# Last four value rows of each expert stage added by VectorE, and the first token tile turned before the last group's rows

## The chip, the core and the metric

One core of a Trainium2 chip runs the whole program once. The metric is device time of one launch in microseconds (us). The kernel before took 2772.89 us (median of three runs, 2770.57 to 2773.94).

## What is computed

Two blocks of a small language model, one after the other, on 256 tokens of width 1024, all in fp32. The first block has two layers; each ends in an expert stage (PEER) and a layer norm, and the change touches only these two ends:

```python
def peer_ffn(x, w_q, subkeys, u_tab, v_tab):          # 8 heads, 16 picks each, 16384 experts
    def block(xb):                                    # 128 tokens
        q = (xb @ w_q).reshape(n, PEER_HEADS, 2, PEER_HALF)
        s = jnp.einsum('nhpc,pkc->nhpk', q, sk)
        ...                                           # two rounds of top-16: eid, softmax weights gw
        u = u_tab[eid]
        act = jax.nn.gelu(jnp.einsum('nhkd,nd->nhk', u, xb))
        coef = gw * act
        return jnp.einsum('nhk,nhkd->nd', coef, v_tab[eid])
...
        y = peer_ffn(x, ...)
        x = layer_norm(DN_ALPHA * x + y, ln2_g[i], ln2_b[i])
```

After layer 0's stage (i = 0) comes the recurrent mixer of layer 1 (`rglru`); after layer 1's stage (i = 1) comes the first feed-forward of the second block (`ffn00`).

## The kernel before

**Tokens and groups.** The 256 tokens are two tiles of 128 (t = 0, 1). An expert stage runs 16 groups j (`NJ`): heads 0 to 7 of token tile 0, then of tile 1. A group has 16 picks k. For each pick one *u row* and one *v row* (128 tokens by 1024 numbers, 512 KB) are gathered by an indirect DMA that POOL issues (`pool_peer`, L1303). Each kind has a ring of 8 slots, so v row g may be issued only when row g - 8 is used up (label `v used g`).

**What each engine does with a row.** VectorE (DVE) takes the dot product of each u row with its token row (`dve_dots`, L1249). The token rows of tile 1 stand in PSUM, in banks 0 and 1 of `ps` (`x_row`). From 16 dots (in the last group: the first 8, then the other 8) come the GELU on ScalarE (ACT, L1154), the coefficients on DVE (`dve_coef`, L1262), and one 128x128 diagonal matrix per pick on ACT (`diag`, L1160). TensorE (PE) multiplies the diagonal by the v row into `acc` (`pe_peer`, L293): two halves of 512 columns, each fp32 product shown as two matmuls, so 4 matmuls in the trace per row.

**Order at the end of a stage.** POOL issues the v rows of a group mostly one group late; rows 8 to 15 of group 15 come after its last u row. PE works through rows 0 to 15 of group 15 in order. At k = 10 it turns token tile 0 of the next step (`pe_tokens`, 8 transposes, L1535), which was normalised in group 12. After row 15, DVE adds the sum to tile 1 (`dve_ln_sum`, L512), takes mean and variance, scales (L517 to L526), and PE turns tile 1. Before that, for i = 1, ACT and DVE make what the feed-forward needs of tile 0: high and low halves (L1544, L1554), the split of the first two weight chunks (L315, L323), and the mean square with its root (L1509, L1512, L1517).

**Order of weight loads.** SyncE (SP) loads weights in a fixed order; `r.x2` (i = 0) and `w1.00.1` (i = 1) are held until row 6 of group 15 is used (`HELD`).

**PSUM tiles.** All short-lived results of PE go through `open_tile`, which deals out the four banks of `ps` in turn: the tile number modulo 4 is the bank, and PE waits until the tile four numbers back has been read.

```python
i = len(tiles)
if i >= BANKS:
    pe.wait_ge(*by("read " + tiles[i - BANKS]))
```

Tiles opened ahead of group 15 of layer 0, by the code: setup 13 (`mem` 4, `kv0` 2, `x0` 4, `par`, `sd`, `sk`), the first mixer 40 (`m.gates`, `m.xq`, `m.0` to `m.5`, `m.col`, 8 of `m.G` and `m.S`, `m.6` to `m.11`, `xs0` 4, `m.N` 4, `xpT0` 4, `my` 3, `xo0` 2), tokens of `xp0` 4, `kv1` 2, and `pq0`/`ps0` 20 (heads 0 and 1 once for each token tile, heads 2 to 7 once): 79. From there to group 15 of layer 1 are 55 more: tokens of `xrt` 4, the second mixer 25 (`r.x` 4, `r.g` 8, `r.xq`, `r.gate` 4, `xs1` 4, `xpT1` 4) with `xo1` 2, tokens of `xp1` 4, `pq1`/`ps1` 20. The last four of a stage are heads 6 and 7 (`pq`, `ps`), long read by then.

Of the kernel before, what the change touches and what calls it, by code (L numbers as in the profile page):

```python
# [179 lines left out]
def build(nc, A, out, known):  # L180
# [9 lines left out]
    with ctx:  # L190
# [23 lines left out]
        def count_of(label):  # L214
            return by(label)[1]
# [54 lines left out]
        def open_tile(name):  # L270
# [5 lines left out]
            tile_bank[name] = i % BANKS  # L276
            return ps[:, i % BANKS, :]

        def tile_of(e, name):

            engine_of[e.who].wait_ge(pe_steps, count_of("tile " + name))
            return ps[:, tile_bank[name], :]
# [214 lines left out]
        def act_attention_out(i, m0):  # L497

            for pair in range(2):
# [7 lines left out]
        ln_bn, ln_ag, ln_std = (stat[:, 0:24].rearrange("p (t a b) -> p t a b", t=2, a=2),  # L507
                                stat[:, 24:28].rearrange("p (t b) -> p t b", t=2), stat[:, 28:30])

        def dve_ln_sum(t):  # L510

            dve.scalar_tensor_tensor(x_tok[:, t, :], x_tok[:, t, :], ALPHA, acc_rows(t), ALU.mult, ALU.add).then_inc(dve_steps, VE.step())  # L512
# [36 lines left out]
        def dve_peer_ln(i, t, part):  # L549

            g, b = f"ln2g{i}", f"ln2b{i}"
            if part == 0:
                dve.wait_ge(pe_steps, count_of(f"v used {PR_K * (NJ * i + PR_HEADS * (t + 1)) - 1}"))
                dve_ln_sum(t)
                dve.wait_ge(dve_steps, VE.n)
                found[f"acc peer{i} read"] = (VE.who, VE.n)
            elif part == 1:
                dve_ln_stats(t)
                dve.wait_ge(dve_steps, VE.n)
                dve.bn_aggr(ln_ag[:, t, :], ln_bn[:, t, :, :].rearrange("p a b -> p (a b)")).then_inc(dve_steps, VE.step())  # L560
                dve.wait_ge(dve_steps, VE.n)
                dve.tensor_scalar(ln_std[:, t:t + 1], ln_ag[:, t, 1:2], LN_EPS, None, ALU.add).then_inc(dve_steps, VE.step(f"var peer{i}.{t}"))
            elif part == 2:
                dve_ln_centred(t, g)
            else:
                dve.wait_ge(act_steps, count_of(f"std peer{i}.{t}"))
                dve.reciprocal(ln_std[:, t:t + 1], ln_std[:, t:t + 1]).then_inc(dve_steps, VE.step())
                dve.wait_ge(dve_steps, VE.n)
                dve_ln_scaled(t, b, f"x peer{i}.{t}")
                dve.wait_ge(dve_steps, VE.n)  # L570
                found[f"row {b}"] = (VE.who, VE.n)
                found[f"x peer{i}"] = (VE.who, VE.n)
                found[f"x {('xrt', 'ffn00')[i]}.{t}"] = (VE.who, VE.n)
# [463 lines left out]
        ex, dots, gel, coef = small(22968, 2, PR_K), small(23000, 2, PR_K), small(23032, 2, PR_K), small(23064, 2, PR_K)  # L1037
        nmx, sm = small(23096, 2, 1), small(23098, 2, 1)
        NJ = TT * PR_HEADS

        def scores(i, o, h, ts):

# [19 lines left out]
        def pe_peer(i):  # L1062
            pe_head_of_tile(i, 1, 0)
            if i == 0:
                pe_memory_keys(1)
                pe_memory_values(1)
            pe_tokens(f"xp{i}", 1)
            pe_head_of_tile(i, 0, 1)
            release(f"wq{i}.0")

            def query(h):

                w = chunk(f"wq{i}.{h}", TE)
                pe_columns(f"pq{i}.{h}", w, x_fm)
                release(f"wq{i}.{h}")

            def query_scores(h):

                pe.wait_ge(act_steps, count_of(f"read pq{i}.{h}"))
                o = open_tile(f"ps{i}.{h}")  # L1080
                scores(i, o, h, range(TT)).then_inc(pe_steps, TE.step(f"tile ps{i}.{h}"))

            for j in range(NJ):
                t = j // PR_HEADS
                if j == PR_HEADS:
                    pe.wait_ge(dve_steps, count_of(f"u used {PR_K * (NJ * i + j) - 1}"))
                for k in range(PR_K):
                    if j == 0 and k == 8:
                        query(2)
                        query_scores(2)  # L1090
                    if j + 3 < PR_HEADS and k == (4 if j else 10):
                        query(j + 3)
                    if j + 3 < PR_HEADS and k == (10 if j else 14):
                        query_scores(j + 3)
                    if j == 1 and k == 12:
                        pe_head_of_tile(i, 1, 1)
                        release(f"wq{i}.1")
                    if j == NJ - 1 and k == 10:
                        pe_tokens(("xrt", "ffn00")[i], 0)
                    g = PR_K * (NJ * i + j) + k  # L1100
                    pe.wait_ge(act_steps, count_of(f"diag {i}.{j}.{k}"))
                    pe.wait_ge(sems[f"v_rows{g % V_SLOTS}"], 16 * (g // V_SLOTS + 1))
                    for half in range(2):
                        ins = mm(acc[:, 2 * t + half, :], diag[:, k, :], v_ring[:, g % V_SLOTS, 512 * half:512 * half + 512],
                                 j % PR_HEADS == 0 and k == 0, j % PR_HEADS == PR_HEADS - 1 and k == PR_K - 1)
                    ins.then_inc(pe_steps, TE.step(f"v used {g}"))
            found[f"acc peer{i}"] = (TE.who, TE.n)

        def coef_part(j, k):

            if 0 < j < NJ - 1:
                return slice(0, PR_K), ""
            return (slice(0, 8), " first") if k < 8 else (slice(8, PR_K), "")

        def act_peer(i):
            def numerators(j):
# [31 lines left out]
            for j in range(NJ):  # L1148
                b = j % 2
                for k in range(PR_K):  # L1150
                    picks, part = coef_part(j, k)
                    if k == picks.start:
                        act.wait_ge(dve_steps, count_of(f"dots {i}.{j}{part}"))
                        act.activation(gel[b][:, picks], dots[b][:, picks], ACT.Gelu).then_inc(act_steps, AC.step(f"gelu {i}.{j}{part}"))  # L1154
                        act.wait_ge(dve_steps, count_of(f"coef {i}.{j}{part}"))
                        if j == PR_HEADS + 2:
                            act_sqrt(f"peer{i}.0", ln_std[:, 0:1])
                    if j:
                        act.wait_ge(pe_steps, count_of(f"v used {PR_K * (NJ * i + j - 1) + k}"))
                    act.activation(diag[:, k, :], ident[:, :], ACT.Copy, scale=coef[b][:, k:k + 1]).then_inc(act_steps, AC.step(f"diag {i}.{j}.{k}"))  # L1160
                if j == 0:
                    read_head(2)
                    numerators(1)
                if j + 3 < PR_HEADS:
                    read_head(j + 3)
                    if j == 1:
                        read_head_of_tile(1, 1)
                    if j + 3 == PR_HEADS - 1:
                        act_x_row(i, 1)
                if j + 2 < NJ:  # L1170
                    numerators(j + 2)

        def dve_topk(out_v, out_i, s):

# [77 lines left out]
        def dve_coef(i, j, k=0):  # L1252
# [10 lines left out]
                dve_steps, VE.step(f"coef {i}.{j}{part}"))  # L1263
            dve.wait_ge(dve_steps, VE.n)

        def dve_peer(i):
            dve_select(i, 0)
            dve_mix_ln(i, 1)
            for j in range(NJ):
                if j == NJ - 1:  # L1270
                    dve_coef(i, j - 1)
                dve_dots(i, j, 0, 2)
                if 0 < j < NJ - 1:
                    dve_coef(i, j - 1, 8 if j == 1 else 0)
                dve_dots(i, j, 2, 4)
                if PR_HEADS + 2 <= j < PR_HEADS + 5:
                    dve_peer_ln(i, 0, (0, 2, 3)[j - PR_HEADS - 2])
                dve_dots(i, j, 4, 8)
                if j in (0, NJ - 1):
                    dve_dots(i, j, 8, 10)  # L1280
                    dve_coef(i, j)
                if j + 1 < NJ:
                    dve_select(i, j + 1)
                if j == PR_HEADS + 2:
                    dve_peer_ln(i, 0, 1)
                dve_dots(i, j, 10 if j in (0, NJ - 1) else 8, PR_K)
            dve_coef(i, NJ - 1, 8)
            if i == DEPTH - 1:
                dve_halves("ffn00", 0)
                for name in ffn_chunks(0, 0)[:2]:  # L1290
                    dve_split(name)
                dve_root("ffn00", 0)
            for part in range(4):
                dve_peer_ln(i, 1, part)
# [1304 lines left out]
        def _(_):  # L2599
# [5 lines left out]
            for i in range(DEPTH):  # L2605
# [4 lines left out]
                    act_rglru()  # L2610
                act_sqrt(f"mix{i}.0", ln_std[:, 0:1])
                act_peer(i)
                if i == 0:
                    act_plain("xrt", 0)
                else:
                    act_square_mean("ffn00", 0, junk_f)
                    act_halves("ffn00", 0)
                    for name in ffn_chunks(0, 0)[:2]:
                        act_split(name)
                act_sqrt(f"peer{i}.1", ln_std[:, 1:2])  # L2620
            act.wait_ge(pe_steps, count_of("acc peer1"))
            for name in ffn_chunks(0, 0)[2:4]:
# [84 lines left out]
```

## Time and profile before

| | us |
|---|---|
| median of three runs | 2772.89 |
| lowest, highest | 2770.57, 2773.94 |
| the profiled execution, whole | 2770.78 |
| its span, first to last instruction | 2769.0 |

Layer 0's expert stage runs from about 191 to 884 us of the span, layer 1's from about 1013 to 1701 us. Times in rows are from the span's start. A timeline row merges instructions that follow without a gap; the bracket is the idle time of that engine just ahead of it and what ended it.

### The profile page before, as it was taken

What the parts mean: (1) busy time and instruction counts of PE and PEld (TensorE: products, weight loads), DVE (VectorE), ACT (ScalarE), POOL (GpSimd) and SP (SyncE); (2) the same over time, 40 slices, a digit from 0 to 9 for tenths busy, and PEclk for the clock granted to TensorE, in tenths of its full rate; (3) what the DMA queues carried; (4) which work ended last, traced back from release to release, by engine and by line L of the source; (5) the groups of instructions that cost most, each with busy time, mean ns of one, the idle gap of its engine ahead of it and who ended that gap; (6) DMA issues with size and microseconds to landing.
All of it is one profiled execution on the core that took longest, in us unless ns stands there. A gap on an engine that the chain in (4) does not pass through costs nothing.

```text
span 2769.0 us, 26764 instructions
## 1 busy us (share of the span) xinstructions
PE 2453.3 (89%) x9068; PEld 1573.6 (57%) x9068; DVE 1641.0 (59%) x3322; ACT 896.5 (32%) x1766; POOL 1109.8 (40%) x1239
## 2 busy tenths in 40 slices
PE   8998978777779988888777778999899999999999
PEld 6865533222324755443222225887877878886787
DVE  1257657667663557666767755556665555557553
ACT  1122221221211521122122114445754454446543
POOL 0016667777774026677777772003600000025000
PEclk9999999999999999999999999999999999999999
DMA  7359999999998459999999997556045555541553
GB/s 235 121 176 394 401 404 409 409 409 402 409 409 305 136 201 395 401 409 409 409 409 404 409 409 277 182 198 173 3 145 169 196 175 183 198 151 65 181 182 122
DMA packets 322199, 766.68 MB, mean 277 GB/s; under 512 B 22064, under 2 KB 172496, under 8 KB 322064
## 3 DMA queue, kind: packets, MB, share of 16 engines
q0 software_dynamic: 150208, 546.77, 50.0%
q1 hardware_dynamic: 170576, 217.69, 24.1%
q8 instruction: 74, 1.21, 0.2%
q10 hardware_dynamic: 1280, 0.50, 0.1%
q14 instruction: 61, 0.50, 0.1%
HBM read 763.83 MB, written 1.05 MB: 276 GB/s over the span
## 4 chain that ended last, share of the span: by engine, by line
PE 47%; DMA 21%; DVE 14%; POOL 9%; issue 6%; ACT 3%; ACTq 0%; DVEq 0%; POOLq 0%
PE ps L293 29%; DMA arena<-in_peer_u,arena 17%; PE acc L293 16%; POOL arena L1303 7%; DVE arena L1249 4%; DMA arena<-in_peer_v,arena 4%; DVE arena L1178 1%; DVE arena L1184 1%; DVE arena L1180 1%; DVE arena L1182 1%; DVE arena L1176 1%; PE ps L1648 1%; ACT hi_ring L315 1%; DVE arena L1212 0%; DVE arena L1216 0%
## 5 line engine op out<-in xcount | busy, mean ns | idle before, releaser
L293 PE MATMUL acc<-arena 128*128 128x512 f32 (+2 forms) x2206 | 1026.0, 609 | 241.3 <-DMA arena<-in_peer_v,arena 139.1
L293 PEld LDWEIGHTS acc<-arena 128*128 128x128 f32 x2206 | 412.2, 199 | 834.4 <-issue 659.0
L1303 POOL DMA_INDIRECT arena<-in_peer_u,arena x512 | 484.1, 946 | 365.9 <-DVE arena L1222 172.7
L1303 POOL DMA_INDIRECT arena<-in_peer_v,arena x512 | 484.4, 946 | 185.8 <-issue 133.4
L1249 DVE CUSTOM_DVE_ANT_0 arena<-arena,ps 128x1024 f32<-128x1024 f32 x256 | 306.6, 1219 | 223.0 <-DMA arena<-in_peer_u,arena 221.1
L1249 DVE CUSTOM_DVE_ANT_0 arena<-arena,acc 128x1024 f32<-128x1024 f32 x256 | 305.7, 1219 | 181.8 <-DMA arena<-in_peer_u,arena 179.6
L323 DVE TENSOR_TENSOR lo_ring<-ring,hi_ring 128x2048 fp32r<-128x2048 f32 x136 | 310.2, 2291 | 166.5 <-ACT hi_ring L315 163.2
L293 PE MATMUL ps<-x_fm,ring 128*128 128x256 f32 (+4 forms) x1792 | 352.7, 359 | 7.7 <-ACT x_fm L1574 2.6
L293 PEld LDWEIGHTS ps<-x_fm,ring 128*128 128x128 f32 (+2 forms) x1792 | 303.4, 189 | 62.3 <-issue 11.7
L293 PE MATMUL ps<-hi_ring,x_hi 128*128 128x512 f32 x704 | 285.5, 406 | 11.8 <-DVE k_mem L1757 6.8
L315 ACT CAST hi_ring<-ring 128x2048 fp32r<-128x2048 f32 x136 | 258.1, 1911 | 70.6 <-DMA ring<-in_ffn_w 70.5
L293 PE MATMUL ps<-hi_ring,x_lo 128*128 128x512 f32 x704 | 276.4, 393 | 0.0
L293 PE MATMUL ps<-lo_ring,x_hi 128*128 128x512 f32 x704 | 274.4, 390 | 0.0
L1160 ACT ACTIVATE arena<-ident,arena 128x128 f32<-128x128 f32 x512 | 153.4, 387 | 143.4 <-DVE arena L1262 143.4
L293 PEld LDWEIGHTS ps<-hi_ring,x_hi 128*128 128x128 f32 x704 | 132.8, 189 | 39.9 <-DVE k_mem L1757 8.4
L293 PEld LDWEIGHTS ps<-hi_ring,x_lo 128*128 128x128 f32 x704 | 132.1, 188 | 30.9
L293 PEld LDWEIGHTS ps<-lo_ring,x_hi 128*128 128x128 f32 x704 | 133.0, 189 | 25.7 <-issue 0.5
L293 PE MATMUL acc<-hi_ring,a_hi 128*128 128x512 f32 x352 | 139.4, 396 | 0.0
L293 PE MATMUL acc<-hi_ring,a_lo 128*128 128x512 f32 x352 | 138.0, 392 | 0.0
L293 PE MATMUL acc<-lo_ring,a_hi 128*128 128x512 f32 x352 | 138.0, 392 | 0.0
L1726 ACT ACTIVATE v_mem<-ps,stat 128x256 f32<-128x256 f32 x88 | 41.9, 476 | 264.8 <-PE ps L293 264.8
L1154 ACT ACTIVATE arena<-arena 128x16 f32<-128x16 f32 (+1 forms) x36 | 7.7, 214 | 369.7 <-DVE arena L1249 369.7
(383 smaller groups left out, 2301.3 us busy)
## 6 DMA issues: line engine op xcount, KB each, us to landing
ring<-in_ffn_w SPq DMA_DIRECT2D x132, 1024.0 KB, 5.5
ring<-in_peer_w_q SPq DMA_DIRECT2D x16, 1024.0 KB, 5.7
ring<-in_mlstm_w_in SPq DMA_DIRECT2D x12, 1024.0 KB, 5.3
arena<-in_peer_u,arena POOLq DMA_INDIRECT x512, 10.7
arena<-in_peer_v,arena POOLq DMA_INDIRECT x512, 11.0
ring<-in_cv_w_in SPq DMA_DIRECT2D x8, 1024.0 KB, 5.8
ring<-in_rglru_w_in SPq DMA_DIRECT2D x8, 768.0 KB, 11.3
ring<-in_w_out SPq DMA_DIRECT2D x5, 1024.0 KB, 5.0
```

Of the source, the lines that this page charges most:

```text
L293: return pe.matmul(o, l, r, start=first, stop=last)
L315: act.copy(parts(name)[0], flat(name, ring, slot)).then_inc(act_steps, AC.step("hi " + name))
L323: dve.tensor_tensor(lo, flat(name, ring, slot), hi.bitcast(F32), ALU.subtract).then_inc(dve_steps, VE.step("lo " + name))
L1160: act.activation(diag[:, k, :], ident[:, :], ACT.Copy, scale=coef[b][:, k:k + 1]).then_inc(act_steps, AC.step(f"diag {i}.{j}.{k}"))
L1176: dve.max(out_v[:, a], s).then_inc(dve_steps, VE.step())
L1178: dve.max_index(out_i[:, a], out_v[:, a], s).then_inc(dve_steps, VE.step())
L1180: dve.match_replace(s, out_v[:, a], s, NEG).then_inc(dve_steps, VE.step())
L1182: dve.max(out_v[:, b], s).then_inc(dve_steps, VE.step())
L1184: dve.max_index(out_i[:, b], out_v[:, b], s).then_inc(dve_steps, VE.step())
L1249: dve.tensor_tensor_reduce(r, r, x_row(t), 1.0, 0.0, ALU.mult, ALU.add, dots[b][:, k:k + 1]).then_inc(dve_steps, VE.step(f"u used {g}"))
L1303: pool.indirect_dma_start(ring_[:, g % slots, :], None, table, bass.IndirectOffsetOnAxis(ix[j % 4][:, k:k + 1].bitcast(U32), 0), element_o ...
L1726: act.activation(sg[:, i % 4, :], o[:, 0:256], ACT.Silu, scale=ssq[:, t:t + 1]).then_inc(act_steps, AC.step(f"silu {n}.{i}"))
```

## The change

1. Rows 12 to 15 of group 15 (`DVE_FROM = 12`) get no diagonal and no matmul. DVE multiplies each by its coefficient and adds it onto token tile 1 in place (`dve_value_rows`), and it is DVE's step that frees their ring slots.
2. Tile 1 has been multiplied by `ALPHA` by ACT at the end of group 12, so the sum of tile 1 becomes a plain addition (`dve_ln_joined`), and it waits for the last row that PE summed (`v summed`).
3. Token tile 0 of the next step is turned by PE ahead of row 0 of group 15, no longer at k = 10. Banks 0 and 1 still hold token rows that the dots read, so `past_token_rows` first adds names to the list of tiles until the next number is 2 modulo 4. Their `read` label is DVE's last dot of the group.
4. ACT's work on that tile (`act_first_tile`) stands between its diagonals 0 to 7 and the second GELU of group 15; for i = 1, DVE's halves and splits stand between the dots of picks 11 to 14. The junk of the square goes to `sc`.

```diff
+        def past_token_rows(i):
+            while len(tiles) % BANKS != 2:
+                name = f"token rows {i}.{len(tiles) % BANKS}"
+                tile_bank[name] = len(tiles) % BANKS
+                tiles.append(name)
...
+        def dve_ln_joined(t):
+            dve.tensor_tensor(x_tok[:, t, :], x_tok[:, t, :], acc_rows(t), ALU.add).then_inc(dve_steps, VE.step())
...
             if part == 0:
-                dve.wait_ge(pe_steps, count_of(f"v used {PR_K * (NJ * i + PR_HEADS * (t + 1)) - 1}"))
-                dve_ln_sum(t)
+                dve.wait_ge(pe_steps, count_of(f"v summed {i}.{t}"))
+                if t:
+                    dve_ln_joined(t)
+                else:
+                    dve_ln_sum(t)
...
-                    if j == NJ - 1 and k == 10:
+                    if j == NJ - 1 and k == 0:
+                        past_token_rows(i)
                         pe_tokens(("xrt", "ffn00")[i], 0)
+                    if on_dve(j, k):
+                        continue
...
+        def act_first_tile(i):
+            if i == 0:
+                act_plain("xrt", 0)
+            else:
+                act_halves("ffn00", 0)
+                act.wait_ge(dve_steps, count_of(f"ix {i}.{NJ - 1}"))
+                for name in ffn_chunks(0, 0)[:2]:
+                    act_split(name)
+                act_square_mean("ffn00", 0, sc[:, 0, 0:D])
...
                     picks, part = coef_part(j, k)
+                    if j == NJ - 1 and k == 8:
+                        act_first_tile(i)
...
+                if j == NJ - 4:
+                    act.activation(x_tok[:, 1, :], x_tok[:, 1, :], ACT.Copy, scale=ALPHA).then_inc(act_steps, AC.step(f"x scaled {i}"))
...
+        def dve_value_rows(i):
+            j = NJ - 1
+            dve.wait_ge(act_steps, count_of(f"x scaled {i}"))
+            for k in range(DVE_FROM, PR_K):
+                g = PR_K * (NJ * i + j) + k
+                dve.wait_ge(sems[f"v_rows{g % V_SLOTS}"], 16 * (g // V_SLOTS + 1))
+                dve.scalar_tensor_tensor(x_tok[:, 1, :], v_ring[:, g % V_SLOTS, :], coef[j % 2][:, k:k + 1], x_tok[:, 1, :],
+                                         ALU.mult, ALU.add).then_inc(dve_steps, VE.step(f"v used {g}"))
+                dve.wait_ge(dve_steps, VE.n)
...
-                dve_dots(i, j, 10 if j in (0, NJ - 1) else 8, PR_K)
-            dve_coef(i, NJ - 1, 8)
+                dve_dots(i, j, 10 if j in (0, NJ - 1) else 8, 12 if j == NJ - 1 else PR_K)
             if i == DEPTH - 1:
                 dve_halves("ffn00", 0)
-                for name in ffn_chunks(0, 0)[:2]:
-                    dve_split(name)
+            dve_dots(i, NJ - 1, 12, 13)
+            if i == DEPTH - 1:
+                dve_split(ffn_chunks(0, 0)[0])
+            dve_dots(i, NJ - 1, 13, 14)
+            if i == DEPTH - 1:
+                dve_split(ffn_chunks(0, 0)[1])
+            dve_dots(i, NJ - 1, 14, PR_K)
+            for bank in range(BANKS):
+                found[f"read token rows {i}.{bank}"] = (VE.who, VE.n)
+            dve_coef(i, NJ - 1, 8)
+            dve_value_rows(i)
+            if i == DEPTH - 1:
                 dve_root("ffn00", 0)
...
-                if i == 0:
-                    act_plain("xrt", 0)
-                else:
-                    act_square_mean("ffn00", 0, junk_f)
-                    act_halves("ffn00", 0)
-                    for name in ffn_chunks(0, 0)[:2]:
-                        act_split(name)
```

## Rows read from the trace of the kernel before

**Rows 1.** The page: span, the chain that ended last by line.

```profile
span 2769.0 us, 26764 instructions
PE ps L293 29%; DMA arena<-in_peer_u,arena 17%; PE acc L293 16%; POOL arena L1303 7%; DVE arena L1249 4%; DMA arena<-in_peer_v,arena 4%; DVE arena L1178 1%; DVE arena L1184 1%; DVE arena L1180 1%; DVE arena L1182 1%; DVE arena L1176 1%; PE ps L1648 1%; ACT hi_ring L315 1%; DVE arena L1212 0%; DVE arena L1216 0%
```

**Rows 2.** Timeline of PE, end of layer 0's stage: start us, length us, instructions [idle <-releaser].

```profile
851.70 3.67 PE L293 MATMUL acc<-arena 128*128 128x512 f32 x8 [0.17 <-DMA arena<-in_peer_v,arena]
...
867.06 5.39 PE L293 MATMUL acc<-arena 128*128 128x512 f32 x12 [0.62 <-DMA arena<-in_peer_v,arena]
...
873.15 10.47 PE L293 MATMUL acc<-arena 128*128 128x512 f32 x24
883.46 3.66 PE L293 MATMUL ps<-x_fm,ring 128*96 128x128 f32 x32
889.35 1.13 PE L1535 MATMUL ps<-ident,x_tok 128*128 128x128 f32 x8 [2.24 <-DVE x_tok L526]
```

**Rows 3.** Timeline of DVE, the same stretch.

```profile
865.66 1.22 DVE L1249 CUSTOM_DVE_ANT_0 arena<-arena,ps 128x1024 f32<-128x1024 f32 x1 [1.33 <-DMA arena<-in_peer_u,arena]
...
883.74 1.22 DVE L512 SCALAR_TENSOR_TENSOR x_tok<-x_tok,acc 128x1024 f32<-128x1024 f32 x1 [16.34 <-PE acc L293]
```

**Rows 4.** Timeline of POOL, the same stretch: gathers of v rows 7, 8 and 15.

```profile
854.33 0.94 POOL L1303 DMA_INDIRECT arena<-in_peer_v,arena  x1 [0.30 <-issue]
855.58 0.93 POOL L1303 DMA_INDIRECT arena<-in_peer_v,arena  x1 [0.30 <-PE acc L293]
...
869.28 0.94 POOL L1303 DMA_INDIRECT arena<-in_peer_v,arena  x1 [1.63 <-PE acc L293]
```

**Rows 5.** Line L1303, issue to landing: last gather of layer 0, of layer 1, all 1024.

```profile
DMA to landing us min/median/max: 9.7/9.7/9.7
...
DMA to landing us min/median/max: 10.2/10.2/10.2
...
DMA to landing us min/median/max: 4.8/10.8/18.9
```

**Rows 6.** Timeline of PE, end of layer 1's stage and the start of the feed-forward.

```profile
1684.47 5.39 PE L293 MATMUL acc<-arena 128*128 128x512 f32 x12 [0.60 <-DMA arena<-in_peer_v,arena]
...
1706.76 1.09 PE L1535 MATMUL ps<-ident,x_tok 128*128 128x128 f32 x8 [1.60 <-DVE x_tok L526]
...
1718.62 0.47 PE L293 MATMUL ps<-hi_ring,x_hi 128*128 128x512 f32 x1 [2.48 <-DVE k_mem L1757]
```

**Rows 7.** Timeline of DVE, the same stretch.

```profile
1675.41 1.22 DVE L1249 CUSTOM_DVE_ANT_0 arena<-arena,ps 128x1024 f32<-128x1024 f32 x1 [2.61 <-DMA arena<-in_peer_u,arena]
...
1691.60 2.16 DVE L1554 SCALAR_TENSOR_TENSOR x_lo<-ps,col,x_hi 128x128 fp32r<-128x128 f32 x8 [6.79 <-ACT x_hi L1544]
1694.32 4.49 DVE L323 TENSOR_TENSOR lo_ring<-ring,hi_ring 128x2048 fp32r<-128x2048 f32 x2 [0.56 <-ACT hi_ring L315]
1698.73 0.15 DVE L1517 RECIPROCAL stat<-stat 128x1 f32<-128x1 f32 x1
1701.15 1.22 DVE L512 SCALAR_TENSOR_TENSOR x_tok<-x_tok,acc 128x1024 f32<-128x1024 f32 x1 [2.26 <-PE acc L293]
```

**Rows 8.** Timeline of ACT: second GELU of group 15, layer 1, and its diagonals.

```profile
1684.35 0.21 ACT L1154 ACTIVATE arena<-arena 128x8 f32<-128x8 f32 x1 [16.43 <-DVE arena L1249]
```

**Rows 9.** Timeline of POOL, layer 1: the last gather.

```profile
1686.70 0.94 POOL L1303 DMA_INDIRECT arena<-in_peer_v,arena  x1 [1.62 <-PE acc L293]
```

**Rows 10.** Groups of DVE by form: busy us, mean ns of one, idle before.

```profile
L526 DVE SCALAR_TENSOR_TENSOR x_tok<-x_tok,stat,rowb 128x1024 f32<-128x1024 f32 x8 | 10.3, 1284 | 0.3
```

**Rows 11.** Timeline of PE: the first rows of layer 1's stage, after an idle stretch.

```profile
1034.03 8.62 PE L293 MATMUL acc<-arena 128*128 128x512 f32 x16 [4.87 <-ACT arena L1160]
```

**Rows 12.** Timeline of DVE and POOL, group 10 of layer 0.

```profile
659.33 1.28 DVE L521 SCALAR_TENSOR_TENSOR x_tok<-x_tok,stat,rowb 128x1024 f32<-128x1024 f32 x1
659.45 1.98 POOL L1303 DMA_INDIRECT arena<-in_peer_u,arena  x1 [0.30 <-DVE arena L1249]
```

**Rows 13.** Stretches: length, busy us of engines, granted clock, DMA share, GB/s.

```profile
1719.71:1723.13 3.42, 3.42 (x10) 2.64 (x9) 1.35 (x2) 0.00 (x0) 0.00 (x0) 0.50 1.10 359
```

More of the change, by code:

```diff
@@ L1039, in build, with on_dve @@
         NJ = TT * PR_HEADS
+        DVE_FROM = 12
+        def on_dve(j, k):
+            return j == NJ - 1 and k >= DVE_FROM
         def scores(i, o, h, ts):
@@ L1104, in pe_peer @@
                         ins = mm(acc[:, 2 * t + half, :], diag[:, k, :], v_ring[:, g % V_SLOTS, 512 * half:512 * half + 512],
-                                 j % PR_HEADS == 0 and k == 0, j % PR_HEADS == PR_HEADS - 1 and k == PR_K - 1)
+                                 j % PR_HEADS == 0 and k == 0, (j, k) in ((PR_HEADS - 1, PR_K - 1), (NJ - 1, DVE_FROM - 1)))
                     ins.then_inc(pe_steps, TE.step(f"v used {g}"))
+                    found[f"v summed {i}.{t}"] = (TE.who, TE.n)
             found[f"acc peer{i}"] = (TE.who, TE.n)
@@ L1157, in act_peer @@
                             act_sqrt(f"peer{i}.0", ln_std[:, 0:1])
+                    if on_dve(j, k):
+                        continue
                     if j:
```

## The prediction

> **What bounds the kernel now.** I read the page first. The chain that ended last goes through u and v rows and PE's sums into `acc` [rows 1], so the expert stages count, but the change touches only their last 30 us, once in each layer. So I read the timelines of PE, DVE, POOL and ACT there. Up to row 7 of group 15 PE waits for v rows (idle <-DMA); from row 7 on it doesn't wait any more [rows 2, 6]. In layer 0 rows 7 to 9 and 10 to 15 take 5.39 and 10.47 us, so a row costs 10.47 / 6 = 1.74 us, and DVE starts the sum of tile 1 at 883.74, after idling 16.34 us for PE [rows 2, 3]. In layer 1 the sum starts at 1701.15, after 2.26 us of waiting for PE [rows 7]. What follows hangs on that sum: in layer 0 the second turning starts 889.35 - 883.74 = 5.61 us later, in layer 1 1706.76 - 1701.15 = 5.61 us [rows 2, 3, 6, 7]. So at both places a microsecond of the sum's start is a microsecond of the kernel, and the terms are the two new starts.
>
> **The value rows on DVE.** Four rows leave PE (4 x 1.74 = 7 us of its tail). On DVE a row is a product and sum with two SBUF inputs of 128x1024; the nearest rows are L521 and L526, 1.28 us each [rows 10, 12]. Gathers come in slower than that, so DVE waits for each, and what counts is when the last one lands. Four diagonals fall away on ACT, off the path.
>
> **Layer 1.** The last gather is issued at 1686.70 and lands 10.2 us later, 1696.9 [rows 5, 9]. Add 1.28 us for its row, some 0.05 for two waits, and the root that now stands there (0.15, with its wait 0.2) [rows 7, 10]: the sum starts at 1698.4. Is all else ready? PE: row 7 from 1684.47, five rows at 1.74 give 1693.2 [rows 6]. ACT: it idles 16.43 us between the diagonals 0 to 7 and the second GELU [rows 8]; the first tile's work (8 copies, two casts, a square with its root) lies today, with 8 diagonals, between 1684.56 and DVE's reciprocal at 1698.73, which is 14.2 us [rows 7, 8], so it fits. The GELU's table has to be loaded again behind the root; I let the 2.2 us that are left cover it, and if they don't, it delays PE's rows 8 to 11, which have 3.7 us to spare ahead of the last landing. DVE: the halves (2.16) and two splits (4.49) fall between dots that each have 1.3 to 2.6 us of waiting for DMA [rows 3, 7]; they overrun by about half a microsecond, against five of slack ahead of the first value row. Turning tile 0 ahead of row 0 costs PE 1 us where it waits for DMA anyway; without that cover it would cost the 1 us. **Term: 1698.4 - 1701.15 = -2.7 us.**
>
> **Layer 0: the turning waits for the dots.** The tile numbers decide this. 79 tiles are open ahead of group 15, and 79 modulo 4 is 3. So `past_token_rows` adds three names, for banks 3, 0 and 1, and the turned tile takes numbers 82 and 83. Number 83 waits until number 79 has been read, which is the added name for bank 3, and its label is DVE's last dot of the group. Bank 3 holds no token row, but PE waits all the same. In layer 1 there are 79 + 3 + 55 = 137 ahead, which is 1 modulo 4: one name for bank 1, and both halves wait for tiles long read. So in layer 0 alone, PE stands ahead of row 0 from about 852 to the end of the last dot, 865.66 + 1.22 = 866.9 [rows 2, 3]. Queued behind it are the rows 0 to 11 of the group; POOL's gathers of rows 8 to 15 wait for rows 0 to 7; the held weights `r.x2` for row 6; ACT's second copy of the tile, and behind it the second GELU. There is no standstill: all u rows and v rows 0 to 7 are issued by 855.3 without a row of this group used [rows 4].
>
> PE then: half a turning, about 0.7 us (8 transposes take 1.13 [rows 2]), and from 867.6 twelve rows, 12 x 1.74 = 20.9 us. It comes from 15 us of idling, so it starts slow: after a shorter idle stretch of 4.87 us, 16 matmuls (four rows) took 8.62 us against 4 x 1.74 = 7.0 [rows 11], so 1.6 us more. Row 11 ends at about 890.1.
>
> Gathers: today row 15 is issued 869.28 - 867.06 = 2.2 us after PE starts row 7 [rows 2, 4]. PE will start row 7 at 867.6 + 1.6 + 7 x 1.74 = 881.4, so row 15 is issued at 883.6. Today it lands 9.7 us after that, behind a queue and beside weight loads; the shortest of the stage is 4.8 [rows 5]. The queue will have drained, because PE hands out one slot in 1.74 us, but the held weights still start just then. I take 6 us, nearer to the empty queue. One more thing shows in the trace: a gather issued beside a two-input DVE instruction took 1.98 us, not 0.94 [rows 4, 12], and DVE's first value row falls on this issue: up to 1 us, of which I take 0.3. Landing 889.9, its row until 891.2. **Term: 891.2 - 883.74 = +7.5 us**; with 4.8 PE sets the end, +6.4; with 9.7 and the full microsecond, +11.8.
>
> The Trainium skill has a rule for that port ("SBUF — State Buffer", section "Who interferes with whom"): a VectorE instruction with two SBUF inputs contends with a GpSimd instruction that reads SBUF, and the later of the two is fully blocked until the first is done. By it, the two splits that now run beside gathers in layer 1 would each hold one gather by up to a split; the trace agrees on the kind, with 1.98 against 0.94 us, and no run shows a split beside a gather.
>
> **Clock.** In layer 1 PE idled 2.48 us ahead of 1718.62, and then its granted clock was 0.50 for 3.4 us, in which it was busy throughout [rows 6, 13]: 1.7 us lost. The change lengthens PE's idling ahead of the second turning (1.60 us today [rows 6]), because PE is done with its rows 8 us earlier and the turning comes only 2.7 us earlier; so the products there run slow and fill the later 2.48 us. Whether the later slow stretch then falls away I can't read; from 0 to -1.7, I take half, **-0.9 us**.
>
> **Nothing else.** ACT's multiplication by ALPHA stands where ACT waits for dots; in layer 0 DVE gets no other work between dots. Token rows and weights used after the sum have landed by then.
>
> **Sum.** +7.5 - 2.7 - 0.9 = +3.9 us. Against the profiled execution (span 2769.0, whole 2770.78) that is 2774.7; it lies 2.1 below the median of 2772.89, and against the median the sum is 2776.8. I say 2776. That is 0.1%, and 0.2% (5.5 us) is about what a measurement of this kernel can tell from no change.
>
> **Rivals.**
> - *Slower: the last gather of layer 0 lands as late as today.* If the held weights beside it, and not the queue, make the 9.7 us, the layer costs +11.8, the sum is +8.2 and the time 2781. It decides from a landing some 8 us after issue. For it: the weights start with the same row. Against: today three or four gathers are in flight ahead, then one. Chance 0.25.
> - *Slower by a little: the splits beside the gathers in layer 1* (the page's rule) delay the landing of the last one by some 2 us, so that layer gives -0.7: sum +5.9, time 2778.5. Against: row 15 is issued only when row 7 is used, 4 us behind the second split. Chance 0.08.
> - *Faster: the added names don't bind in layer 0*, for instance because I miscounted tiles. Then the last gather lands at 869.28 + 9.7 = 879.0 [rows 4, 5], the sum starts at 880.3, and the layer gives -3.4; with -2.7 and -0.9 that is -7.0: 2766. Chance 0.07.
> - *Forecast* as above, 2773 to 2779 by its own bounds: 0.60.
>
> **Range and chances.** The range reaches from 2770 (clock luck on top of the forecast) to 2781, which leaves out the faster case and the worst of the slow one. Faster by over 0.2%: 0.06, from the third rival. Slower by over 0.2%: 0.25 + 0.05, from the first two and the forecast's upper edge. Within: 0.64.
>
> **What would show it.** Layer 0: PE idle for about 15 us ahead of row 0 of group 15 with DVE L1249 as releaser, or (third rival) none; then 48 matmuls without a gap, and v gathers issued 1.7 us apart. DVE's plain addition at 891 there, or at 880. The last landing 6 or 10 us after issue. Layer 1: the addition at about 1698.4 less the shift, just after the fourth value row, not after PE. Value rows of 1.28 us. I would be wrong above all if PE's wait isn't there, or if something other than the last gather and PE's rows sets the sum in layer 0.

## The result and the profile after

The changed kernel took 2778.41 us (median of 20 runs, 2773.33 to 2783.51). The kernel before, run on the same chips, took 2770.20 us (median of 20, 2766.01 to 2774.32; the three runs shown ahead of the prediction all lie in the upper half of these). The ratio is 1.0030, interval 1.0024 to 1.0036: slower by 0.3%, some 8 us. The profiled execution took 2778.40 us, 7.6 us over the profiled execution before (2770.78); its span is 2776.7.

The end of layer 0's stage, PE in the changed kernel (compare rows 2). In all timelines: start us, length us, instruction, count, [idle ahead <-what ended it].

```profile
852.49 0.60 PE L1595 MATMUL ps<-ident,x_tok 128*128 128x128 f32 x4
868.00 1.12 PE L1595 MATMUL ps<-ident,x_tok 128*128 128x128 f32 x4 [14.91 <-DVE arena L1289]
868.91 22.25 PE L300 MATMUL acc<-arena 128*128 128x512 f32 x48
891.00 3.66 PE L300 MATMUL ps<-x_fm,ring 128*96 128x128 f32 x32
899.74 1.97 PE L1595 MATMUL ps<-ident,x_tok 128*128 128x128 f32 x8 [5.08 <-DVE x_tok L537]
902.47 22.71 PE L300 MATMUL ps<-x_fm,ring 128*96 128x128 f32 x112 [0.77 <-ACT x_fm L1634]
```

The turning is cut in two. Its second half waits 14.91 us for L1289, which is the dots. Behind it stand twelve rows in one piece (48 matmuls). The same stretch on DVE (compare rows 3):

```profile
866.71 1.22 DVE L1289 CUSTOM_DVE_ANT_0 arena<-arena,ps 128x1024 f32<-128x1024 f32 x1 [1.30 <-DMA arena<-in_peer_u,arena]
...
885.88 2.61 DVE L1313 SCALAR_TENSOR_TENSOR x_tok<-arena,x_tok 128x1024 f32<-128x1024 f32 x2 [15.78 <-DMA arena<-in_peer_v,arena]
891.21 1.28 DVE L1313 SCALAR_TENSOR_TENSOR x_tok<-arena,x_tok 128x1024 f32<-128x1024 f32 x1 [2.72 <-DMA arena<-in_peer_v,arena]
892.80 1.28 DVE L1313 SCALAR_TENSOR_TENSOR x_tok<-arena,x_tok 128x1024 f32<-128x1024 f32 x1 [0.32 <-DMA arena<-in_peer_v,arena]
894.12 1.22 DVE L519 TENSOR_TENSOR x_tok<-x_tok,acc 128x1024 f32<-128x1024 f32 x1
```

The value rows (L1313) take 1.28 us each, and the plain addition (L519) follows the fourth without idling: the last gather sets it, not PE, whose rows were done at 891. POOL (compare rows 4 and 5), the first gather that waits for PE and the last one, with the last one's time to landing:

```profile
872.55 0.94 POOL L1363 DMA_INDIRECT arena<-in_peer_v,arena  x1 [15.92 <-PE acc L300]
...
884.57 0.94 POOL L1363 DMA_INDIRECT arena<-in_peer_v,arena  x1 [0.78 <-PE acc L300]
...
DMA to landing us min/median/max: 8.1/8.1/8.1
```

The end of layer 1's stage (compare rows 6 and 7), PE's row 7, then DVE's last value row, root and addition:

```profile
1695.64 8.82 PE L300 MATMUL acc<-arena 128*128 128x512 f32 x20 [0.57 <-DMA arena<-in_peer_v,arena]
...
1708.03 1.28 DVE L1313 SCALAR_TENSOR_TENSOR x_tok<-arena,x_tok 128x1024 f32<-128x1024 f32 x1 [0.43 <-DMA arena<-in_peer_v,arena]
1709.35 0.16 DVE L1577 RECIPROCAL stat<-stat 128x1 f32<-128x1 f32 x1
1709.55 1.22 DVE L519 TENSOR_TENSOR x_tok<-x_tok,acc 128x1024 f32<-128x1024 f32 x1
```

Absolute times are shifted by what happened earlier (the changed program's first dot of layer 0 already came 1.45 us later, in code that is the same). So the two ends are compared by distances. In layer 0: from the start of the group's last dot to the sum. In layer 1: from PE's start on row 7, which begins when its gather lands, to the sum (the last dot itself moves there).

| | before | after | change |
|---|---|---|---|
| layer 0, last dot to sum | 18.08 | 27.41 | +9.33 |
| layer 1, row 7 to sum | 16.68 | 13.91 | -2.77 |

Two smaller terms lie behind the sums. From the sum of layer 0 to PE's row 7 of layer 1 the changed kernel takes 0.8 us more (801.52 against 800.73), and from the sum of layer 1 to the start of the third unit of the feed-forward 0.25 us more (17.72 against 17.47). Together 9.33 + 0.8 - 2.77 + 0.25 = 7.6 us, as much as lies between the two executions. That they agree so closely is partly luck: the changed kernel was already 1.05 us late at that last dot of layer 0 (866.71 against 865.66), and behind the third unit, in code that is the same, it won as much back.

### The profile page after: what moved, and what is told of

The parts are those of the page before. It is cut to its first block, busy times and chain, and to the rows that moved or that the text cites. A ratio compares the mean times of both kernels' runs of the same rounds, so it can differ in the third digit from the quotient of the medians.

```text
span 2776.7 us, 26706 instructions
## 1 busy us (share of the span) xinstructions
PE 2440.6 (88%) x9036; PEld 1570.2 (57%) x9036; DVE 1653.0 (60%) x3330; ACT 899.7 (32%) x1762; POOL 1116.5 (40%) x1239
## 3 DMA queue, kind: packets, MB, share of 16 engines
HBM read 763.83 MB, written 1.05 MB: 275 GB/s over the span
## 4 chain that ended last, share of the span: by engine, by line
PE 50%; DMA 19%; DVE 14%; POOL 8%; issue 5%; ACT 3%; ACTq 0%; DVEq 0%; POOLq 0%
PE ps L300 30%; PE acc L300 18%; DMA arena<-in_peer_u,arena 14%; POOL arena L1363 7%; DMA arena<-in_peer_v,arena 5%; DVE arena L1289 5%; DVE arena L1218 1%; DVE arena L1224 1%; DVE arena L1220 1%; DVE arena L1222 1%; DVE arena L1216 1%; PE ps L1708 1%; DMA ring<-in_peer_w_q 1%; ACT hi_ring L322 1%; PE ps L1595 1%
## 5 line engine op out<-in xcount | busy, mean ns | idle before, releaser
L300 PE MATMUL acc<-arena 128*128 128x512 f32 (+2 forms) x2174 | 1008.8, 607 | 242.2 <-DMA arena<-in_peer_v,arena 138.6
L300 PEld LDWEIGHTS acc<-arena 128*128 128x128 f32 x2174 | 405.8, 199 | 824.6 <-issue 646.8
L1289 DVE CUSTOM_DVE_ANT_0 arena<-arena,ps 128x1024 f32<-128x1024 f32 x256 | 306.5, 1220 | 216.7 <-DMA arena<-in_peer_u,arena 215.9
L1289 DVE CUSTOM_DVE_ANT_0 arena<-arena,acc 128x1024 f32<-128x1024 f32 x256 | 305.5, 1220 | 180.0 <-DMA arena<-in_peer_u,arena 178.3
```

Source lines behind the costliest of these rows:

```text
L300: return pe.matmul(o, l, r, start=first, stop=last)
L1289: dve.tensor_tensor_reduce(r, r, x_row(t), 1.0, 0.0, ALU.mult, ALU.add, dots[b][:, k:k + 1]).then_inc(dve_steps, VE.step(f"u used {g}"))
```

## The experiments

Each was timed beside the kernel before. The first four ran on one chip, the last two on another.

**1. Layer 0 without the wait (e1_bank3).** The name added for bank 3 counts as read at the start of the group. Banks 0 and 1, which hold the token rows, keep their label.

```diff
                 if j == NJ - 1:
                     dve_coef(i, j - 1)
+                    for bank in (2, 3):
+                        found[f"read token rows {i}.{bank}"] = (VE.who, VE.n)
...
-            for bank in range(BANKS):
+            for bank in range(2):
                 found[f"read token rows {i}.{bank}"] = (VE.who, VE.n)
```

> The changed kernel, but the name added for bank 3 counts as read at the start of group 15, so that the turning in layer 0 no longer waits for the last dot. Theory (that wait is the cost): layer 0 now gains like layer 1; the sum there starts right behind the fourth value row, about 3 us earlier than before instead of 9 us later, and layer 1 keeps its -2.7 us: together -5 to -6 us against the kernel before, about 2765 us. Rival (the value rows on VectorE or the order of ACT and VectorE cost it): the time stays near 2778 us.

Measured: 2764.82 us (12 runs), ratio 0.9982 (0.9972 to 0.9991), 5.3 us faster than before. PE and DVE in layer 0:

```profile
850.55 1.04 PE L1597 MATMUL ps<-ident,x_tok 128*128 128x128 f32 x8
851.42 9.09 PE L300 MATMUL acc<-arena 128*128 128x512 f32 x20
861.12 1.96 PE L300 MATMUL acc<-arena 128*128 128x512 f32 x4 [0.60 <-DMA arena<-in_peer_v,arena]
...
878.24 1.28 DVE L1313 SCALAR_TENSOR_TENSOR x_tok<-arena,x_tok 128x1024 f32<-128x1024 f32 x1 [0.24 <-DMA arena<-in_peer_v,arena]
879.55 1.22 DVE L519 TENSOR_TENSOR x_tok<-x_tok,acc 128x1024 f32<-128x1024 f32 x1
```

The eight transposes come in one piece, and from the sixth row on PE waits for DMA again. From the last dot (864.85) to the sum are 14.70 us, 3.38 less than before. One label is worth 27.41 - 14.70 = 12.7 us at this place.

**2. The change in layer 1 alone (e2_layer1).** Layer 0 as before: turning at k = 10, all rows on PE.

```diff
-            return j == NJ - 1 and k >= DVE_FROM
+            return i == 1 and j == NJ - 1 and k >= DVE_FROM
...
-                    if j == NJ - 1 and k == 0:
+                    if i == 1 and j == NJ - 1 and k == 0:
                         past_token_rows(i)
-                        pe_tokens(("xrt", "ffn00")[i], 0)
+                        pe_tokens("ffn00", 0)
+                    if i == 0 and j == NJ - 1 and k == 10:
+                        pe_tokens("xrt", 0)
```

> The change in layer 1 alone; layer 0 as in the kernel before. Theory: -2.7 us from the sum of layer 1 and nothing else, about 2767.5 us, 0.1% below the kernel before. Rival (value rows, splits between dots or gathers held beside splits cost time): no gain or a loss, 2770 us or more.

Measured: 2766.32 us (11 runs), ratio 0.9985 (0.9976 to 0.9994), 3.8 us faster. Row 7 to sum is 1697.57 - 1683.82 = 13.75 us, 2.93 less than before; layer 0 keeps its 18.07. So in layer 1 the change as a whole is a gain, with the value rows on DVE and the work between dots in it.

**3. The value rows back on PE (e3_rows_on_pe).** Turning and work on the first tile stay ahead; the wait in layer 0 stays.

```diff
-            return j == NJ - 1 and k >= DVE_FROM
+            return False and j == NJ - 1 and k >= DVE_FROM
...
-            dve_value_rows(i)
```

> The changed kernel with rows 12 to 15 left on TensorE in both layers; only the turning and the work on the first tile are ahead, the wait in layer 0 is there. Theory: in layer 0 sixteen rows instead of twelve stand behind the wait, so the sum starts about 4 us later than in the changed kernel (13 us later than before), and in layer 1 only the turning's 0.9 us leaves the tail: about +12 us, 2782 us. Rival (the value rows on VectorE cost it): 2770 us or less.

Measured: 2784.37 us (6 runs), ratio 1.0051 (1.0038 to 1.0064), 14.3 us slower. PE and DVE, layer 0:

```profile
867.43 1.11 PE L1591 MATMUL ps<-ident,x_tok 128*128 128x128 f32 x4 [14.91 <-DVE arena L1286]
868.34 29.34 PE L300 MATMUL acc<-arena 128*128 128x512 f32 x64
...
897.79 1.22 DVE L523 SCALAR_TENSOR_TENSOR x_tok<-x_tok,acc 128x1024 f32<-128x1024 f32 x1 [28.25 <-PE acc L300]
```

The same wait, now with sixteen rows behind it, and PE sets the sum: last dot (866.14) to sum 31.65 us, +13.57 against before, of the 13 expected. In layer 1 row 7 to sum is 15.80, -0.88, about what the eight transposes cost that stood there (in the kernel before, 1690.57 - 1689.69 = 0.88): that is the turning alone. So part 3 of the change loses 13.6 us in layer 0, and the value rows on DVE bring 4.2 of them back (27.41 against 31.65).

**4. The held weights later (e4_hold).**

```diff
-        HELD = {"r.x2": TT * PR_HEADS * PR_K - 10, ...
+        HELD = {"r.x2": TT * PR_HEADS * PR_K - 5, ...
```

> The changed kernel with the weights of layer 1's mixer held until row 11 of group 15 of layer 0 is used, not row 6. Theory (weight loads delay the last gather by some 2 us): the last gather lands about 6 us after its issue instead of 8.1, the sum of layer 0 starts about 2 us earlier, at the end of TensorE's rows: 2776.5 us. Rival (the landing is long for another reason): landing and time as in the changed kernel, 2778.4 us.

Measured: 2776.56 us (11 runs), ratio 1.0023 (1.0014 to 1.0031); its interval overlaps that of the changed kernel (1.0024 to 1.0036), so the times alone do not part the two. The traces do. The last gather's time to landing, and DVE:

```profile
DMA to landing us min/median/max: 6.3/6.3/6.3
...
884.70 3.93 DVE L1313 SCALAR_TENSOR_TENSOR x_tok<-arena,x_tok 128x1024 f32<-128x1024 f32 x3 [15.60 <-DMA arena<-in_peer_v,arena]
889.80 1.28 DVE L1313 SCALAR_TENSOR_TENSOR x_tok<-arena,x_tok 128x1024 f32<-128x1024 f32 x1 [1.18 <-DMA arena<-in_peer_v,arena]
891.12 1.22 DVE L519 TENSOR_TENSOR x_tok<-x_tok,acc 128x1024 f32<-128x1024 f32 x1
```

8.1 us to landing became 6.3, and last dot (865.71) to sum is 25.41 us, 2.0 less than in the changed kernel. In both, three earlier gathers are still in flight when the last one is issued, so the weights are what differs. In experiment 3, where the weights start with row 6 as in the changed kernel, it took 8.3.

**5. PE kept busy ahead of the second turning (e6_bank3_warm).** Experiment 1, with small products whose results are overwritten, at both places.

```diff
-    ... half * RG_D:half * RG_D + RG_D], RG_D)
+    ... half * RG_D:half * RG_D + RG_D], RG_D, warm=48)
...
-                        pe_tokens(n, 1)
+                        pe_tokens(n, 1, 48 if n == "ffn00" else 0)
```

> The kernel of e1_bank3, with 48 small matmuls on the identity (256 columns, results overwritten) ahead of the wait for the second turning, at both places, so that TensorE isn't idle there. Theory (the longer idle stretch costs clock): in e1_bank3 the granted clock is 0.50 from 883.5 to 893.7 us, of which TensorE works about 8.6 us at half speed, so some 4 us come back in layer 0, less in layer 1, where TensorE waits later anyway: 4 to 5 us below e1_bank3, about 2760.5 us. Rival (the slow stretch lies beside other waits): as e1_bank3, 2764.8 us.

Measured: 2762.98 us (8 runs), ratio 0.9974 (0.9963 to 0.9984). It is the fastest kernel here, 7.9 us below the kernel before (2770.87 beside it), but its interval overlaps that of experiment 1, and the 4 to 5 us did not come. PE in layer 0, first in experiment 1, then here:

```profile
885.17 1.97 PE L1597 MATMUL ps<-ident,x_tok 128*128 128x128 f32 x8 [6.61 <-DVE x_tok L537]
887.90 27.26 PE L300 MATMUL ps<-x_fm,ring 128*96 128x128 f32 x128 [0.77 <-ACT x_fm L1636]
```

```profile
879.23 5.40 PE L300 MATMUL ps<-ident 128*128 128x256 bf16 x48
885.98 1.09 PE L1597 MATMUL ps<-ident,x_tok 128*128 128x128 f32 x8 [1.34 <-DVE x_tok L537]
887.88 24.36 PE L300 MATMUL ps<-x_fm,ring 128*96 128x128 f32 x120 [0.82 <-ACT x_fm L1636]
```

From the turning's start to the next products 1.90 us instead of 2.73, so the turning ran at full clock. A slow stretch still came right behind it, but a shorter one. Granted clock (third number from the end) in the slow stretch of experiment 1 and in that of this kernel:

```profile
883.47:893.71 10.24, 7.78 (x35) 7.41 (x36) 2.02 (x6) 5.44 (x7) 1.06 (x2) 0.50 0.33 108
```

```profile
887.96:891.38 3.42, 3.42 (x17) 3.42 (x18) 0.00 (x0) 3.36 (x5) 0.00 (x0) 0.50 0.45 167
```

The products behind the turning ran 893.71 - 887.90 = 5.8 us at 0.50 there and 3.4 us here, half of the difference being 1.2 us; with the turning's 0.8 that is 2.0 us, and by DVE's first copy of their result this kernel is indeed 2.0 us ahead (12.93 us after the sum, against 14.93). Later in the layer 1.1 us of it goes, at another slow stretch that lasted 6.8 us instead of 3.4. In layer 1 nothing came: row 7 to sum is 13.82 against 13.81, and though the products behind the turning start 0.8 us sooner, DVE's first result of the feed-forward (`k_mem`) comes 17.10 us after the sum in both. The expectation took 8.6 us as worked at half speed, where the row above shows 7.78, and took all of the stretch as avoidable.

**6. Two value rows instead of four (e7_from14).** Experiment 1 with one constant changed.

```diff
-        DVE_FROM = 12
+        DVE_FROM = 14
```

> The kernel of e1_bank3 with two value rows on VectorE (14 and 15) instead of four. Theory (the landing of the last gather sets the sum): TensorE ends two rows later, 3.5 us, which is still at or just ahead of the last value row, so the time stays within 0.5 us per layer of e1_bank3, 2765 us. Rival (each row that leaves TensorE's tail is worth its 1.74 us): 7 us above e1_bank3, 2772 us.

Measured: 2766.85 us (11 runs), ratio 0.9982 (0.9972 to 0.9993), the ratio of experiment 1. DVE in layer 0:

```profile
879.21 1.29 DVE L1313 SCALAR_TENSOR_TENSOR x_tok<-arena,x_tok 128x1024 f32<-128x1024 f32 x1 [10.30 <-DMA arena<-in_peer_v,arena]
880.78 1.28 DVE L1313 SCALAR_TENSOR_TENSOR x_tok<-arena,x_tok 128x1024 f32<-128x1024 f32 x1 [0.29 <-DMA arena<-in_peer_v,arena]
882.10 1.22 DVE L519 TENSOR_TENSOR x_tok<-x_tok,acc 128x1024 f32<-128x1024 f32 x1
```

Last dot (867.18) to sum 14.92 us against 14.70, row 7 to sum 14.10 against 13.81. Two rows that went back to PE cost 0.2 and 0.3 us, not 3.5. Layer 1 by the number of value rows, row 7 to sum: none 15.80 (experiment 3), two 14.10, four 13.81 (experiment 1). With two, the sum already follows the last landing, so two more bring little.

## Why the prediction was right, and where its sizes were off

**The range and the side.** 2776 was said, 2770 to 2781, and 2778.4 came. That the number is only 2.4 us off is partly luck: it was built on the median of three runs, 2772.89, and over 20 runs the kernel before takes 2770.20. The change itself was forecast as +3.9 us and came as +8.2. The likeliest class, within 0.2%, did not come; slower by more than 0.2% did, which had 0.30. The terms:

| term | said | measured |
|---|---|---|
| layer 0, sum | +7.5 (6.4 to 11.8) | +9.33 |
| layer 1, sum | -2.7 | -2.77 |
| clock (measured: all behind the sums) | -0.9 | +0.8 and +0.25 |
| all | +3.9 | +7.6 by these rows, +8.2 by the medians |

**Layer 0, the wait: shown.** The count of tiles was right. PE idled 14.91 us with the dots as releaser (15 said), half a turning and 48 matmuls followed, and the rows took 22.25 us (20.9 + 1.6 said). Experiment 1 takes only the wait away and the loss turns into a gain.

**Layer 0, the last landing: the step that was mis-sized.** The last gather was to land 6 us after its issue; it took 8.1. The estimate took the value nearer to an empty queue, with one gather in flight ahead. By their issues and landings three were (those issued at 879.42, 881.13 and 882.85, landed at 885.8, 887.1 and 891.1), and six, not three or four, in the kernel before. The held weights start with row 6, and with them out of the way the landing took 6.3 us with three ahead as well (experiment 4). So the 6 us would have been about right without the weights, and the weights added some 2 us. The first rival had this mechanism, with its threshold at a landing 8 us after issue; it came half way, 8.1 and not 9.7. That its sum, +8.2, is also what the medians show is luck: layer 0's sum cost 9.33 of its 11.8 us, and the clock went the other way. The microsecond for a gather held beside a value row did not come: the last gather's issue took 0.94 us, because the first value row started at 885.88, after that issue.

**Layer 1: shown.** The sum follows the last value row and the root directly. Experiments 1, 2 and 4 give 13.8, 13.75 and 14.1 us from row 7, of 16.68 before.

**The splits beside the gathers (the second rival).** Its mechanism is there and its price is not. POOL in layer 1 of the changed kernel, gathers of rows 11 and 12, and DVE's splits:

```profile
1688.54 2.31 POOL L1363 DMA_INDIRECT arena<-in_peer_v,arena  x1 [0.30 <-issue]
1691.15 3.04 POOL L1363 DMA_INDIRECT arena<-in_peer_v,arena  x1 [0.30 <-issue]
...
1687.75 2.29 DVE L330 TENSOR_TENSOR lo_ring<-ring,hi_ring 128x2048 fp32r<-128x2048 f32 x1
...
1691.09 2.29 DVE L330 TENSOR_TENSOR lo_ring<-ring,hi_ring 128x2048 fp32r<-128x2048 f32 x1
```

Both gathers end 0.81 us after the split that they met. The rule of the Trainium skill ("SBUF — State Buffer", section "Who interferes with whom"), that the later of the two is blocked until the first is done, agrees with these rows. It costs nothing here: the last gather waits for row 7 anyway, and landed 10.1 us after its issue, before 10.2 [rows 5].

**Clock: wrong in sign for this execution.** The slow stretch in the feed-forward that was to fall away in half of the cases came again in the changed kernel's trace (compare rows 13):

```profile
1728.64:1732.05 3.41, 3.41 (x10) 2.66 (x9) 1.08 (x2) 0.00 (x0) 0.00 (x0) 0.50 1.10 349
```

Nor did it come about as said. The second turning started after 6.57 us of idling and ran at the low clock, which was foreseen, but the later idling was not filled: 2.47 us, before 2.48 [rows 6].

```profile
1727.27 0.47 PE L300 MATMUL ps<-hi_ring,x_hi 128*128 128x512 f32 x1 [2.47 <-DVE k_mem L1817]
```

In experiments 1 to 5 the slow stretch did not come; in 1, 2, 4 and 5 layer 1 gained about 4 to 4.5 us from row 7 to DVE's result of the third unit, not 2.5 as in the changed kernel. In experiment 6 one came a little earlier (1715.91 to 1719.32). Experiment 3 had the same 2.47 us of idling and no long idling ahead of the second turning, and the stretch stayed away all the same. So taking half of it was fair, but the reason given for it is not shown.

In layer 0 the 0.8 us are not the second turning's. It starts after 5.08 us of idling (2.24 before) and loses 0.8 us at the low clock (to the next products 902.47 - 899.74 = 2.73 us, before 891.26 - 889.35 = 1.91). But the slow stretch then ends sooner behind it: the products run 906.02 - 902.47 = 3.6 us at 0.50, before 897.10 - 891.26 = 5.8, which gives 1.1 us back. DVE's first copy of their result comes 13.83 us after the sum, before 14.11. The loss comes 80 us behind the sum, where a slow stretch lasted 6.8 us instead of 3.4. The kernel before, then the changed one:

```profile
890.28:897.10 6.82, 6.04 (x30) 5.87 (x28) 0.00 (x0) 5.10 (x7) 0.00 (x0) 0.50 0.41 123
965.37:968.78 3.41, 3.05 (x15) 3.04 (x16) 3.31 (x12) 2.15 (x7) 0.00 (x0) 0.50 0.00 0
```

```profile
899.20:906.02 6.82, 5.52 (x25) 5.15 (x26) 0.89 (x4) 4.79 (x7) 0.53 (x1) 0.50 0.46 156
974.29:981.11 6.82, 5.28 (x24) 4.28 (x25) 5.65 (x15) 4.32 (x14) 0.00 (x0) 0.50 0.06 20
```

Experiment 2, whose layer 0 is the old one, has 6.8 us there too, and experiments 1, 3, 4 and 6 have 3.4. So nothing shows that the change causes this loss.

**Still open.** The medians differ by 8.2 us, the two profiled executions by 7.6. Executions of one kernel spread over 7 to 12 us here, so the remaining half microsecond can't be put anywhere. What decides which slow stretches of the clock an execution has is open too.

## What to carry to other kernels

When a transfer or a turn of buffers is moved ahead, write down which buffer number it gets in every place where the code is used, and what the last reader of that number is: the same lines waited for nothing in one layer and for a whole group in the other, because of 79 modulo 4. Give a name that only keeps a place the reader of that place, not the last reader of its neighbours. And where the last landing sets the end, moving more work off the busy engine behind it buys next to nothing (two more rows 0.2 to 0.3 us here); look at what else is loading in those microseconds.

## What the runs showed of the hardware

In layer 0 of the changed kernel a gather of 512 KB issued with no other in flight landed 4.1 us after its issue (872.55), and one with three ahead of it 6.3 us after (879.42). Weight loads beside it count too: of two gathers with three ahead each, the one issued at 881.13, ahead of the weights, took 6.0 us and the next, issued 0.24 us after the first weight load, 8.3 us. The issue of a gather that met a two-input DVE instruction ended 0.81 us after that instruction, so it took 2.31 and 3.04 us beside the splits instead of 0.94; the slow gather in the kernel before fits this as well (1.98 us, end 0.82 us after L521 [rows 12]). And small products that kept PE at work at full clock for 5.4 us (from 879.23 on, experiment 5) did not keep a stretch at 0.50 from following, from 887.96 on, after two idle gaps of 1.34 and 0.82 us around the turning.
